# A transformer kernel's first layer: retention blocks moved between the k-tiles of the projections

## Chip, cores, metric

The kernel runs on one core of one Trainium2 chip. The metric is the device time in microseconds (us) of one execution; lower is better. It computes in f32, and all weights and activations come from HBM in one launch.

## What is computed

Four layers on 512 tokens of width 1024: two of a first block and two of a second. The change touches the first layer's mixer alone:

```
def _even_mixer(h, w_in, ret_norm_g, hg_norm_g, lb, w_out):
    rq, rk, rv, rg, gq, gf, gi, gg = _split_cols(h @ w_in, EV_SIZES)      # eight times 512 columns
    rq = _rotary(_split_heads(rq, RET_HEADS), pos)                        # 4 heads of 128
    rk = _rotary(_split_heads(rk, RET_HEADS), pos) * (RET_DK ** -0.5)
    ret = _retention_chunkwise(rq, rk, _split_heads(rv, RET_HEADS))
    ret = _merge_heads(_head_layer_norm(ret, ret_norm_g)) * jax.nn.silu(rg.astype(jnp.float32))
    hg = _hgrn2_chunkwise(_split_heads(gq, HG_HEADS), _split_heads(gf, HG_HEADS), _split_heads(gi, HG_HEADS), lb)
    hg = _merge_heads(_head_rms_norm(hg, hg_norm_g)) * jax.nn.silu(gg.astype(jnp.float32))
    y = jnp.concatenate([ret, hg], axis=-1).astype(h.dtype)
    return y @ w_out
```

The retention is `(q k^T * decay) v` over causal blocks of 128 tokens, then a layer norm per head (mean, centred value, mean square). The recurrence (hgrn2) uses forget gates `f = lb + (1 - lb) * sigmoid(gf)`, the running sum of their logarithm, and keys `1 - f`.

## The kernel before

**Units and jobs.** Weights come in units of 1024 x 256 (1 MB). SyncE loads a unit into one of two `raw` buffers; ScalarE (ACT) rounds it to `wH`; VectorE (DVE) subtracts (`wL = raw - wH`). TensorE (PE) then does three passes for each product, `hH wH`, `hL wH` and `hH wL` (`passes`): for a unit of 8 k-tiles and 2 output tiles that is 48 matmuls of 512 columns, called a job. In a token-major unit the operands are swapped: 96 matmuls of 256 columns. A job's result lies in one half of the PSUM tile `G` until DVE has read it (`job_free`). The `step` of ACT waits for the end of job n and rounds the unit of job n+2; the `step` of DVE reads the result of job n, then makes the `wL` of that unit. Every engine works strictly in the order in which its rows stand, and the semaphores that each row waits for are written by hand.

**The first layer's mixer.** Jobs 0 to 11 are twelve units of the projection: queries and keys (with rotary), values (token-major), retention gates RG, recurrent queries GQ, forget gates CUM. Then PE does the retention alone: 16 scores (`psS`, up to 512 columns, plain f32), each multiplied by the decay on DVE into `ws[SD]`, and 16 values blocks into `G`; per head the widths are 512, 384, 256 and 128. After that four means (a matmul with ones), four centred tiles on DVE, squares on ACT, and their sums per token (`stats`, 128x1 matmuls), DVE and GpSimd for the inverse root, four `spread`s (transposes that bring a column to all partitions), of which each needs its `columns` from DVE. Two token-major units of the recurrence's inputs GI stand before and behind the spreads. The level loop follows: 8 levels of recurrence blocks on `psS`, with two-matmul-tile pieces of the units GG between them.

**Bias rows.** After job 3, ACT issues a DMA that writes a table of 2560 KB to HBM for the second layer (`bias_out`).

Of the kernel before, what the change touches and what calls it, by code (L numbers as in the profile page):

```python
# [18 lines left out]
ALU = mybir.AluOpType  # L19
ACT = mybir.ActivationFunctionType  # L20
AX = mybir.AxisListType

P = 128
S = 512
# [165 lines left out]
def program(nc, a, out, scratch):  # L190
    ctx = contextlib.ExitStack()
    with ctx:
# [66 lines left out]
        MEMT, MH, ML = (0, 24), (4, 28), (8, 32)  # L259
        XOL, XOH = 0, 36  # L260
# [19 lines left out]
        for half in (8, 16, 32, 64, 128):  # L280
# [43 lines left out]
                                                     sem("rot_in"))  # L324
        b_done, b_read = sem("b_done"), sem("b_read")
        rs_done, rp_ready = sem("rs_done"), sem("rp_ready")
        mean_done, xc_ready = sem("mean_done"), sem("xc_ready")
# [38 lines left out]
        def _(sp):  # L366
# [16 lines left out]
            with sp.Fori(1, sum(UNITS_1) // 2) as i:  # L383
# [33 lines left out]
        def _(pe):  # L417
# [247 lines left out]
            for l in range(2):  # L665
                if l == 0:
                    for j in range(12):
                        if j == 0:
                            first_jobs(halves_in=True)
                        elif j in (4, 5):  # L670
                            token_major(h_op)
                        elif j > 1:
                            plain(h_op)
                        if j in (2, 3):
                            bias_rows(j - 2)

                    pe.wait_ge(b_read, 2)

                    pe.wait_ge(job_free, c.job.v + 2)
                    for s_ in range(18):  # L680
                        if s_ < 16:
                            h, jb = s_ // 4, s_ % 4

                            wait(pe, rp_ready, s_ - 1)
                            pe.matmul(psS[:, s_ % 2, 0:S - jb * P], ws[:, KR + h, jb * P:jb * P + P],
                                      ws[:, QR + h, jb * P:S], start=True, stop=True).then_inc(rs_done, 1)
                        r = s_ - 2
                        if r >= 0:
                            h, jb = r // 4, r % 4
                            pe.wait_ge(rp_ready, r + 1)  # L690
                            if r % 8 == 0:
                                take_job()
                            mm = pe.matmul(G[:, c.job.p * 2 + h % 2, jb * P:S], ws[:, V0 + jb, h * P:h * P + P],
                                           ws[:, SD + r % 3, 0:S - jb * P], start=(jb == 0), stop=(jb == 3))
                            if r % 8 == 7:
                                end_job(mm)


                    pe.wait_ge(job_free, c.job.v + 2)
                    for h in range(4):  # L700
                        wait(pe, xc_ready, h - 1)
                        pe.matmul(psS[:, h % 2, :], ones[:], ws[:, OS + h, :], start=True, stop=True)\
                            .then_inc(mean_done, 1)
                    pe.wait_ge(xc_ready, 4)
                    for m in range(2):
                        stats("tile", m, npairs=2)
                    token_major(h_op)
                    for h in range(4):
                        spread()
                    token_major(h_op)  # L710

# [425 lines left out]
        def _(act):  # L1137
# [187 lines left out]
            for l in range(2):  # L1325
                if l == 0:
                    for j in range(12):
                        step()
                        if j in (6, 7):
                            in_place(RG + 2 * (j - 6), ACT.Silu)  # L1330
                        elif j in (10, 11):
                            in_place(CUM + 2 * (j - 10), ACT.Sigmoid)
                        if j == 3:
                            bias_exps()
                    act.wait_ge(ln_in, 1)
                    activation(flat(CUM, 4), flat(CUM, 4), ACT.Ln).then_inc(ln_ready, 1)

                    c.job.off += 2
                    for m in range(2):
                        act.wait_ge(xc_ready, 2 * m + 2)  # L1340
                        square(ws[:, XC + 2 * m:XC + 2 * m + 2, :])
                    step()
# [3 lines left out]
                        .then_inc(t4_ready, 1)  # L1346
                    act.wait_ge(tn_ready, c.nrm.v + 4)
                    for h in range(4):
                        activation(ws[:, ZA + h, :], ws[:, CUM + h, :], ACT.Exp)
                        activation(ws[:, ZB + h, :], ws[:, CUM + h, :], ACT.Exp, scale=-1.0).then_inc(he_exp, 1)  # L1350
                    step()
                    step()
# [198 lines left out]
        def _(dve):  # L1551
# [348 lines left out]
            for l in range(2):  # L1900
                if l == 0:
# [31 lines left out]

                    for j in range(12):
                        if j < 4:
                            o = (QR, KR)[j // 2] + 2 * (j % 2)
                            step(rotary(ws[:, o:o + 2, :]))
                        elif j in (4, 5):
                            step(tokens(ws[:, V0:V0 + 4, (j % 2) * 256:(j % 2) * 256 + 256], 1))
                        elif j in (6, 7):  # L1940
                            step(by_rb(RG + 2 * (j - 6)))
                            c.ar.off += 1
                        elif j in (8, 9):
                            step(by_rb(GQ + 2 * (j - 8)))
                        else:
                            step(by_rb(CUM + 2 * (j - 10)))
                            forget(j - 10)
                        if j in (2, 3):
# [6 lines left out]
                    V.memset(tick[:], 0.0).then_inc(ln_in, 1)  # L1955
                    dve.wait_ge(table_in, 16)

                    n_out = 0
                    for s_ in range(17):
                        if s_ < 16:  # L1960
                            h, jb = s_ // 4, s_ % 4
                            w = S - jb * P
                            dve.wait_ge(rs_done, s_ + 1)
                            V.tensor_tensor(ws[:, SD + s_ % 3, 0:w], psS[:, s_ % 2, 0:w], ws[:, DEC + h, 0:w], ALU.mult)\
                                .then_inc(rp_ready, 1)
                        if s_ in (11, 16):
                            step(store(ws[:, OS + 2 * n_out:OS + 2 * n_out + 2, :]), unit=False)
                            n_out += 1
                    for h in range(4):
                        dve.wait_ge(mean_done, h + 1)  # L1970
                        V.scalar_tensor_tensor(ws[:, XC + h, :], psS[:, h % 2, :], -1.0 / P, ws[:, OS + h, :],
                                               ALU.mult, ALU.add).then_inc(xc_ready, 1)

                    def head_norm(src, gain, gate, to=None):
# [16 lines left out]

                    dve.wait_ge(ln_ready, 1)
                    for h in range(4):
                        ins = V.tensor_tensor_scan(ws[:, CUM + h, :], ws[:, RST, :], ws[:, CUM + h, :], 0.0,
                                                   ALU.mult, ALU.add)
                    ins.then_inc(scan_ready, 1)
                    head_norm(XC, lambda h: colx("ret", h), RG, RO)
                    inputs = lambda n: tokens(ws[:, GI:GI + 4, n * 256:n * 256 + 256], 1)
                    step(inputs(0))

                    for h in range(4):
                        dve.wait_ge(he_exp, h + 1)
                        V.tensor_tensor(ws[:, ZA + h, :], ws[:, ZA + h, :], ws[:, GQ + h, :], ALU.mult)
                        V.tensor_tensor(ws[:, ZB + h, :], ws[:, ZB + h, :], ws[:, KEY + h, :], ALU.mult)\
                            .then_inc(hz_ready, 1)
                    dve.wait_ge(t4_ready, 1)
                    for h in range(4):
# [597 lines left out]
```

## Time and profile before

| | |
|---|---|
| median of 3 runs | 3205.85 us (3205.09 to 3208.72) |
| profiled execution, its own time | 3207.22 us |
| its span in the profile | 3205.4 us |
| PE busy / weight loads | 3133.1 us (98%) / 2615.3 us (82%) |
| DVE / ACT / GpSimd busy | 1584.9 / 1075.8 / 290.4 us |
| granted clock of PE, mean | 0.987 |

The span is from the first to the last instruction. A matmul's row is as long as its way through the array, while matmuls come closer together than that; so the distance between starts counts, not the length. The clock is a share of 2.4 GHz.

### The profile page before, as it was taken

Reading aid. Unit: us, or ns where it says so; the run is one execution under the profiler, and the core shown is the slowest. Engines: PE = TensorE matmul, PEld = TensorE weight load, DVE = VectorE, ACT = ScalarE, POOL = GpSimd, SP = SyncE. Lnnn points to the kernel's source line nnn. Section 1 sums busy time; section 2 is a strip of 40 time slices with the busy share of each in tenths; the row PEclk is TensorE's granted clock in tenths of the full one; section 3 lists DMA queues with packets and bytes.
Section 4 is the critical chain, followed back from the end, with each engine's and each line's share of the span. In section 5 each row is a group of like instructions: output and inputs, shape, how many; then the busy total and the mean of one; then the engine's idle time right before and its main releaser. Section 6 shows DMA issues by size and latency. Waiting matters only on the chain.

```text
span 3205.4 us, 38813 instructions
## 1 busy us (share of the span) xinstructions
PE 3133.1 (98%) x15548; PEld 2615.3 (82%) x15548; DVE 1584.9 (49%) x1850; ACT 1075.8 (34%) x1166; POOL 290.4 (9%) x161
## 2 busy tenths in 40 slices
PE   9989999999999899999999999999999999999998
PEld 7778988888889798888888778888888777888887
DVE  7364644554334554455435755444433665444433
ACT  3212433443222443344323332333323342233322
POOL 0011200010000020011000300110100210101100
PEclk9999999999999999999999999999999999999999
DMA  4411411222232131122233122222222312222223
GB/s 167 123 40 48 140 63 66 105 92 105 105 107 92 35 136 67 66 93 104 94 113 104 66 71 100 92 96 101 92 107 97 93 66 101 97 92 92 95 105 115
DMA packets 47721, 299.92 MB, mean 94 GB/s; under 512 B 7091, under 2 KB 7347, under 8 KB 13284
## 3 DMA queue, kind: packets, MB, share of 16 engines
q1 hardware_dynamic: 42480, 288.01, 25.5%
q10 hardware_dynamic: 5108, 10.02, 1.3%
q8 instruction: 98, 1.61, 0.2%
q14 instruction: 35, 0.29, 0.0%
HBM read 293.26 MB, written 4.75 MB: 93 GB/s over the span
## 4 chain that ended last, share of the span: by engine, by line
PE 87%; DVE 6%; ACT 3%; issue 2%; DMA 2%; POOL 0%; ACTq 0%; DVEq 0%; SPq 0%
PE G L437 79%; DMA raw<-in_units 1%; DVE wL L1559 1%; ACT wH L1147 1%; PE psS L732 1%; PE psS L497 1%; DVE mxt L1766 1%; PE G L939 1%; DVE ws L2239 1%; PE psS L932 1%; PE psS L1030 1%; PE G L1039 1%; DVE ws L2236 0%; PE psT L529 0%; PE psS L488 0%
## 5 line engine op out<-in xcount | busy, mean ns | idle before, releaser
L437 PE MATMUL G<-hH,wH 128*128 128x512 f32 x2560 | 1016.3, 397 | 23.5 <-DVE wL L1559 7.9
L437 PE MATMUL G<-hL,wH 128*128 128x512 f32 x2560 | 1002.8, 392 | 0.0
L437 PE MATMUL G<-hH,wL 128*128 128x512 f32 x2560 | 1002.7, 392 | 0.0
L1559 DVE TENSOR_TENSOR wL<-raw,wH 128x2048 fp32r<-128x2048 f32 x265 | 637.7, 2406 | 663.7 <-ACT wH L1147 663.4
L437 PE MATMUL G<-wsr,wH 128*128 128x512 f32 (+1 forms) x2528 | 751.6, 381 | 2.0 <-DVE wsr L2105 0.9
L1147 ACT ACTIVATE wH<-raw 128x2048 fp32r<-128x2048 f32 x265 | 505.7, 1908 | 604.2 <-PE G L437 565.0
L437 PEld LDWEIGHTS G<-hH,wH 128*128 128x128 f32 x2560 | 484.6, 189 | 139.7 <-issue 16.3
L437 PEld LDWEIGHTS G<-hH,wL 128*128 128x128 f32 x2560 | 484.3, 189 | 102.8
L437 PEld LDWEIGHTS G<-hL,wH 128*128 128x128 f32 x2560 | 485.0, 189 | 98.0
L437 PEld LDWEIGHTS G<-wsr,wH 128*128 128x128 f32 x2528 | 466.8, 189 | 95.2 <-DVE wsr L2105 1.8
L437 PE MATMUL G<-wsr,wL 128*128 128x512 f32 (+1 forms) x1264 | 479.1, 379 | 0.0
L437 PEld LDWEIGHTS G<-wsr,wL 128*128 128x128 f32 x1264 | 238.4, 189 | 44.7
L2436 POOL TENSOR_TENSOR wsr<-sq,wsr 128x1024 f32 x44 | 105.8, 2405 | 841.3 <-ACT wsr L1264 841.3
L2414 POOL TENSOR_TENSOR rsb<-ms,neghalf 128x4 f32<-128x4 f32 (+4 forms) x21 | 37.6, 1790 | 1165.2 <-DVE ms L1602 1004.6
L1264 ACT ACTIVATE wsr<-sq 128x1024 f32 x44 | 46.7, 1062 | 231.4 <-DVE sq L1789 231.4
L1233 ACT ACTIVATE ws<-ws,mxt 128x128 f32<-128x128 f32 (+3 forms) x96 | 54.1, 564 | 207.3 <-DVE mxt L1766 206.8
L1713 DVE TENSOR_TENSOR x<-x,G 128x1024 f32<-128x1024 f32 x39 | 47.6, 1221 | 150.3 <-PE G L437 150.3
L437 PE MATMUL G<-wH,hH 128*128 128x256 f32 x384 | 113.5, 295 | 0.0
L437 PE MATMUL G<-wH,hL 128*128 128x256 f32 x384 | 109.8, 286 | 0.0
L437 PE MATMUL G<-wL,hH 128*128 128x256 f32 x384 | 109.7, 286 | 0.0
L1671 DVE TENSOR_TENSOR sq<-G,hmask 128x1024 f32<-128x1024 f32 x44 | 53.8, 1222 | 90.1 <-PE G L437 89.9
L1671 DVE TENSOR_TENSOR tn<-G,hmask 128x1024 f32<-128x1024 f32 x44 | 53.9, 1225 | 87.1 <-PE G L437 86.1
(272 smaller groups left out, 2591.2 us busy)
## 6 DMA issues: line engine op xcount, KB each, us to landing
raw<-in_units SPq DMA_DIRECT2D x265, 1024.0 KB, 4.8
ws<-bias_rows SPq DMA_DIRECT2D x2, 1536.0 KB, 14.7
bias_rows<-ws ACTq DMA_DIRECT2D x1, 2560.0 KB
x<-in_x SPq DMA_DIRECT2D x4, 512.0 KB, 7.9
ws<-in_mem ACTq DMA_DIRECT2D x2, 1024.0 KB, 4.8
ws<-bias_rows ACTq DMA_DIRECT2D x1, 2048.0 KB, 8.2
out_x<-x SPq DMA_DIRECT2D x4, 512.0 KB, 7.7
ws<-in_decay ACTq DMA_DIRECT2D x1, 1280.0 KB, 8.6
```

The source lines that it names most:

```text
L437: mm = pe.matmul(o, mv if swap else wt, wt if swap else mv, start=first and n == 0, stop=last and n == 2)
L497: mm = pe.matmul(st[:, col:col + 1], lhs, ones[:, 0:1], start=True, stop=True)
L732: mm = pe.matmul(psS[:, n % 2, o:o + w], k_[:, ks:ks + P], q_[:, qs:qs + w], start=True, stop=True)
L932: mm = pe.matmul(psS[:, r % 2, 0:M], ws[:, XQ + 2 * h + t, qt * P:qt * P + P], kx[:, 2 * h + t, :], start=(t == 0), stop=(t == 1))
L1147: activation(wH[:, g.p, :], raw[:, g.p, :], ACT.Copy).then_inc(wh_ready, 1)
L1233: return activation(p_, p_, ACT.Exp, bias=mxt[:, r % 4:r % 4 + 1], accum_out=den[:, r % 4:r % 4 + 1])
L1264: activation(aH[:, bass.ds(i * 2, 2), :], sq[:, 1], ACT.Copy).then_inc(ffn_h, 1)
L1559: V.tensor_tensor(wL[:, g.p, :], raw[:, g.p, :], wH[:, g.p, :].bitcast(F32), ALU.subtract)\
L1671: V.tensor_tensor(dst, g, rb_pair, ALU.mult).then_inc(job_free, 1)
L1713: V.tensor_tensor(x[:, 2 * jj:2 * jj + 2, :], x[:, 2 * jj:2 * jj + 2, :], g, ALU.add)\
L2414: W.tensor_tensor(dst[:, 0:cols], ms[:, 0:cols], neghalf[:].to_broadcast([P, cols]), ALU.pow)\
L2436: W.tensor_tensor(aL[:, bass.ds(i * 2, 2), :], sq[:, 1], aH[:, bass.ds(i * 2, 2), :].bitcast(F32), ALU.subtract).then_inc(ffn_ready, 1)
```

## The change

The order of the first layer's units becomes 0 to 5, 10, 11, 8, 9, 6, 7, 12 to 15: the forget gates are jobs 6 and 7, the recurrent queries 8 and 9, the retention gates 10 and 11. The retention no longer stands by itself. In jobs 6 to 9, after every second k-tile, there is a slot with one score and one value block; job 10's four slots hold the last two value blocks and the four means; job 11's second and third hold the sums of squares; the four spreads stand in the first of the two token-major units, after each token tile. The values go to `psT` instead of `G`, copied head by head, so there are two jobs fewer (68). Some temporary tiles are renumbered. On DVE and ACT the rows are put in the matching order.

```diff
-JOBS_1 = (70, 66)
+JOBS_1 = (68, 66)
+ORDER_1 = (0, 1, 2, 3, 4, 5, 10, 11, 8, 9, 6, 7, 12, 13, 14, 15)
-        ZA, ZB, DD, SX2, SX1, RO = 0, 4, 8, 12, 16, 39
+        ZA, ZB, DD, SX2, SX1, RO = 8, 35, 0, 12, 16, 39
@@ tensor
-                    for j in range(12):
+                    for j in range(6):
...
+                    def slotted(slot):
+                        take_unit()
+                        take_job()
+                        for k in range(KT):
+                            for t in range(2):
+                                w0 = k * 256 + t * P
+                                mm = passes(G[:, c.job.p * 2 + t, :], w0, w0 + P, h_op, k, slice(0, S),
+                                            k == 0, k == KT - 1)
+                            if k == KT - 1:
+                                end_job(mm)
+                            if k % 2 == 1:
+                                slot(k // 2)
+                        c.unit.off += 1
...
+                    def retained(s_):
+                        if s_ == 0:
+                            pe.wait_ge(b_read, 2)
+                            pe.wait_ge(job_free, c.job.v)
                         if s_ < 16:
                             h, jb = s_ // 4, s_ % 4
                             wait(pe, rp_ready, s_ - 1)
                             pe.matmul(psS[:, s_ % 2, 0:S - jb * P], ws[:, KR + h, jb * P:jb * P + P],
                                       ws[:, QR + h, jb * P:S], start=True, stop=True).then_inc(rs_done, 1)
                         r = s_ - 2
                         if r >= 0:
                             h, jb = r // 4, r % 4
                             pe.wait_ge(rp_ready, r + 1)
-                            if r % 8 == 0:
-                                take_job()
-                            mm = pe.matmul(G[:, c.job.p * 2 + h % 2, jb * P:S], ws[:, V0 + jb, h * P:h * P + P],
+                            if jb == 0 and h > 1:
+                                pe.wait_ge(os_ready, h - 1)
+                            mm = pe.matmul(psT[:, h % 2, jb * P:S], ws[:, V0 + jb, h * P:h * P + P],
...
+                    for j in range(4):
+                        slotted(lambda n: retained(4 * j + n))
+                    slotted(centred)
+                    slotted(squares)
@@ scalar
+                    for n in range(2):
+                        step()
+                        in_place(CUM + 2 * n, ACT.Sigmoid)
                     act.wait_ge(ln_in, 1)
                     activation(flat(CUM, 4), flat(CUM, 4), ACT.Ln).then_inc(ln_ready, 1)
-                    c.job.off += 2
+                    step()
+                    step()
+                    act.wait_ge(scan_ready, 1)
+                    activation(ws[:, RST, :], flat(CUM, 4).rearrange("p (n l) -> p n l", l=4)[:, :, 3], ACT.Exp)\
+                        .then_inc(t4_ready, 1)
                     for m in range(2):
                         act.wait_ge(xc_ready, 2 * m + 2)
                         square(ws[:, XC + 2 * m:XC + 2 * m + 2, :])
                     step()
+                    in_place(RG, ACT.Silu)
+                    act.wait_ge(os_ready, 4)
+                    act.wait_ge(bias_out, 16)
@@ vector
+                    for s_ in range(4):
+                        decayed(s_)
+                    step(by_rb(CUM))
+                    decayed(4)
+                    decayed(5)
+                    forget(0)
+                    decayed(6)
+                    retained(0)
+                    decayed(7)
+                    step(by_rb(CUM + 2))
...
+                    rstd(2, 16, P)
+                    first = c.bc.off
+                    columns(0)
+                    columns(4)
+                    step(by_rb(RG + 2))
```

How PE's rows stand shows it best. Before, where the retention begins: behind the last matmul of job 11 (line 437) come the scores (L685, from keys and queries in `ws` to `psS`) and the value blocks (L693, to `G`).

```order
L437 MATMUL G<-hH,wL 128x512
L685 MATMUL psS<-ws 128x512
L685 MATMUL psS<-ws 128x384
L685 MATMUL psS<-ws 128x256
L693 MATMUL G<-ws 128x512
L685 MATMUL psS<-ws 128x128
L693 MATMUL G<-ws 128x384
```

In the changed kernel the same place of the retention, score 2 and value block 0, stands in the third slot of job 6 (the unit's matmuls are line 443 there).

```order
L443 MATMUL G<-hH,wL 128x512
L707 MATMUL psS<-ws 128x256
L715 MATMUL psT<-ws 128x512
L443 MATMUL G<-hH,wH 128x512
L443 MATMUL G<-hL,wH 128x512
```

A pair of blocks that had only other blocks around it now has twelve matmuls of the unit before and after it.

DVE's rows in job 7 and its step. Before, the step (L1917 reads `G`, L1559 is the `wL` of the next unit but one) and the forget gates (L1928 to L1932) stand in one piece, ahead of all decay products (L1964).

```order
L1917 TENSOR_TENSOR ws<-G,tn 128x1024
L1559 TENSOR_TENSOR wL<-raw,wH 128x2048
L1928 TENSOR_SCALAR ws<-ws,lbt 128x512 x2
L1931 TENSOR_SCALAR ws<-ws 128x1024
L1932 TENSOR_SCALAR ws<-ws 128x1024
L1955 MEMSET tick 128x1
L1964 TENSOR_TENSOR ws<-psS,ws 128x512
L1964 TENSOR_TENSOR ws<-psS,ws 128x384
```

In the changed kernel, from the `wL` of unit 8 (L1614) to the `wL` of unit 9: decay products (L2008), forget gates (L1983 to L1987), a head's copy (L2014) and the step (L1972) alternate.

```order
L1614 TENSOR_TENSOR wL<-raw,wH 128x2048
L2008 TENSOR_TENSOR ws<-psS,ws 128x512
L2008 TENSOR_TENSOR ws<-psS,ws 128x384
L1983 TENSOR_SCALAR ws<-ws,lbt 128x512 x2
L1986 TENSOR_SCALAR ws<-ws 128x1024
L1987 TENSOR_SCALAR ws<-ws 128x1024
L2008 TENSOR_TENSOR ws<-psS,ws 128x256
L2014 COPY ws<-psT 128x512
L2008 TENSOR_TENSOR ws<-psS,ws 128x128
L1972 TENSOR_TENSOR ws<-G,tn 128x1024
L1614 TENSOR_TENSOR wL<-raw,wH 128x2048
```

The products of scores 4 and 5 stand behind the `wL` of unit 8, and those of 6 and 7 behind the forget gates.

## Rows read from the trace of the kernel before

**Rows 1.** The page: the chain that ended last, by engine.

```profile
PE 87%; DVE 6%; ACT 3%; issue 2%; DMA 2%; POOL 0%; ACTq 0%; DVEq 0%; SPq 0%
```

**Rows 2.** PE's waits, 60 to 345 us: total, times, longest.

```profile
PE psS L685 <- DVE ws L1964: 4.4, 1, 4.4
...
PE psT L529 <- DVE wide L1677: 2.0, 2, 1.2
```

**Rows 3.** PE in order of time, jobs 8 and 10: start, length, [idle before].

```profile
107.23 0.50 PE L437 MATMUL G<-hH,wH 128*128 128x512 f32 x1 [1.60 <-DVE wL L1559]
...
131.45 0.54 PE L437 MATMUL G<-hH,wH 128*128 128x512 f32 x1 [2.16 <-DVE wL L1559]
...
135.20 0.40 PE L437 MATMUL G<-hH,wH 128*128 128x512 f32 x1
```

**Rows 4.** PE in order of time, from job 11's end to the level loop.

```profile
154.72 0.39 PE L437 MATMUL G<-hH,wL 128*128 128x512 f32 x1
...
170.84 1.02 PE L685 MATMUL psS<-ws 128*128 128x512 f32 x2
...
175.16 1.02 PE L685 MATMUL psS<-ws 128*128 128x512 f32 x2
...
181.61 3.89 PE L702 MATMUL psS<-ws,ones 128*128 128x512 f32 x8 [1.32 <-DVE ws L1584]
186.28 3.81 PE L497 MATMUL psS<-ones,sq 128*128 128x1 f32 x32 [0.78 <-DVE ws L1971]
189.96 0.56 PE L437 MATMUL G<-wH,hH 128*128 128x256 f32 x1
...
202.75 0.28 PE L437 MATMUL G<-wH,hL 128*128 128x256 f32 x1
202.87 0.28 PE L437 MATMUL G<-wL,hH 128*128 128x256 f32 x1
...
207.31 0.56 PE L437 MATMUL G<-wH,hH 128*128 128x256 f32 x1
...
220.21 1.95 PE L732 MATMUL psS<-ws 128*128 128x128 f32 x16
```

**Rows 5.** Stretches: length, busy us (x) per engine, granted clock, DMA, GB/s.

```profile
83.69:94.57 10.88, 10.88 (x50) 9.01 (x49) 3.95 (x5) 1.92 (x1) 0.00 (x0) 1.00 0.71 143
...
131.00:144.00 13.00, 12.55 (x48) 10.26 (x49) 3.82 (x3) 1.91 (x1) 0.00 (x0) 0.87 0.45 163
190.00:222.00 32.00, 29.98 (x226) 29.50 (x226) 19.23 (x35) 10.11 (x12) 13.90 (x6) 0.90 0.10 34
```

**Rows 6.** PE in order of time, one cycle of the level loop.

```profile
228.72 1.95 PE L732 MATMUL psS<-ws 128*128 128x128 f32 x16
230.42 0.48 PE L437 MATMUL G<-hH,wH 128*128 128x512 f32 x1
...
231.88 1.95 PE L732 MATMUL psS<-ws 128*128 128x128 f32 x16
```

**Rows 7.** PE in order of time: sums and two spreads in the second layer.

```profile
961.43 1.84 PE L497 MATMUL psS<-ones,sq 128*128 128x1 f32 x16
963.13 1.07 PE L529 MATMUL psT<-ident,wide 128*128 128x128 f32 x8
963.95 0.47 PE L437 MATMUL G<-hH,wH 128*128 128x512 f32 x1
```

**Rows 8.** ACT and DVE in order of time, at the weights, a product, the columns.

```profile
102.93 1.92 ACT L1147 ACTIVATE wH<-raw 128x2048 fp32r<-128x2048 f32 x1 [17.05 <-DMA raw<-in_units]
127.15 1.92 ACT L1147 ACTIVATE wH<-raw 128x2048 fp32r<-128x2048 f32 x1 [17.18 <-DMA raw<-in_units]
...
104.88 2.29 DVE L1559 TENSOR_TENSOR wL<-raw,wH 128x2048 fp32r<-128x2048 f32 x1 [8.87 <-ACT wH L1147]
167.59 0.69 DVE L1964 TENSOR_TENSOR ws<-psS,ws 128x512 f32<-128x512 f32 x1 [1.21 <-PE psS L685]
193.79 0.24 DVE L1677 COPY wide<-rsb 128x4 f32<-128x4 f32 x2 [3.01 <-POOL rsb L2414]
```

More of the change, by code:

```diff
@@ L325, in program @@
         b_done, b_read = sem("b_done"), sem("b_read")
+        rv_done, os_ready = sem("rv_done"), sem("os_ready")
         rs_done, rp_ready = sem("rs_done"), sem("rp_ready")
@@ L382, in _ @@
                 sp.dma_start(dst, s_).then_inc(par_in, 16)
-            with sp.Fori(1, sum(UNITS_1) // 2) as i:
+            for n in range(2, len(ORDER_1)):
+                sp.wait_ge(wl_ready, n - 1)
+                sp.dma_start(raw[:, n % 2, :], a["units"][ORDER_1[n]]).then_inc(raw_in[n % 2], 16)
+            with sp.Fori(len(ORDER_1) // 2, sum(UNITS_1) // 2) as i:
                 for j in range(2):
@@ L699, in _, with mean @@
-                    pe.wait_ge(job_free, c.job.v + 2)
-                    for h in range(4):
-                        wait(pe, xc_ready, h - 1)
+                            if jb == 3:
+                                mm.then_inc(rv_done, 1)
+                    def mean(h):
+                        pe.wait_ge(os_ready, h + 1)
+                        if h < 2:
+                            pe.wait_ge(rp_ready, 16)
+                        else:
+                            pe.wait_ge(xc_ready, h - 1)
@@ L702, in _, with centred @@
                         pe.matmul(psS[:, h % 2, :], ones[:], ws[:, OS + h, :], start=True, stop=True)\
                             .then_inc(mean_done, 1)
[L704 to L710, printed above, removed]
+                    def centred(n):
+                        if n < 2:
+                            retained(16 + n)
+                        mean(n)
@@ new lines, in squares @@
+                    def squares(n):
+                        if n == 1:
+                            pe.wait_ge(xc_ready, 4)
+                        if 1 <= n <= 2:
+                            stats("tile", n - 1, npairs=2)
+                    for j in range(4):
[3 more added lines that the diff above has]
+                    for n in range(2):
+                        take_unit()
+                        take_job()
+                        for tt in range(ST):
+                            for k in range(KT):
+                                mm = passes(G[:, c.job.p * 2 + tt // 2, (tt % 2) * 256:(tt % 2) * 256 + 256],
+                                            k * 256, k * 256 + 256, h_op, k, slice(tt * P, tt * P + P),
+                                            k == 0, k == KT - 1, swap=True)
+                            if tt == ST - 1:
+                                end_job(mm)
+                            if n == 0:
+                                spread()
+                        c.unit.off += 1
@@ L1350, in _ @@
                         activation(ws[:, ZB + h, :], ws[:, CUM + h, :], ACT.Exp, scale=-1.0).then_inc(he_exp, 1)
+                    step()
+                    in_place(RG + 2, ACT.Silu)
+                    step()
                     step()
@@ L1932, in forget @@
                         c.link(V.tensor_scalar(f2, f2, F_FLOOR, None, ALU.max))
-                    for j in range(12):
+                    for j in range(6):
                         if j < 4:
@@ L1937, in _ @@
                             step(rotary(ws[:, o:o + 2, :]))
-                        elif j in (4, 5):
+                        else:
                             step(tokens(ws[:, V0:V0 + 4, (j % 2) * 256:(j % 2) * 256 + 256], 1))
[L1940 to L1947, printed above, removed]
                         if j in (2, 3):
@@ L1954, in _, with decayed, retained, scan @@
                             bias_sums()
[L1955 to L1969, printed above, removed]
+                    def decayed(s_):
+                        h, jb = s_ // 4, s_ % 4
+                        w = S - jb * P
+                        dve.wait_ge(rs_done, s_ + 1)
+                        V.tensor_tensor(ws[:, SD + s_ % 3, 0:w], psS[:, s_ % 2, 0:w], ws[:, DEC + h, 0:w], ALU.mult)\
+                            .then_inc(rp_ready, 1)
+                    def retained(h):
+                        dve.wait_ge(rv_done, h + 1)
+                        V.tensor_copy(ws[:, OS + h, :], psT[:, h % 2, :]).then_inc(os_ready, 1)
+                    def scan(h):
+                        return V.tensor_tensor_scan(ws[:, CUM + h, :], ws[:, RST, :], ws[:, CUM + h, :], 0.0,
+                                                    ALU.mult, ALU.add)
+                    def centred(h):
                         dve.wait_ge(mean_done, h + 1)
@@ L2005, in _ @@
                             .then_inc(hz_ready, 1)
+                    step(inputs(0))
                     dve.wait_ge(t4_ready, 1)
```

63 lines of the change are left out of this document (40 added, 23 removed).

## The prediction

> **What bounds the kernel now.** I read the chain of work that ended last first: 87% of it is TensorE (PE) [rows 1]. PE's busy share there is not news; what matters is what PE's time consists of where the change is made. So I next read who makes PE wait between 60 and 345 us, then PE's instructions in order of time, and at the end the other engines' rows at the places where PE waits.
>
> Two places lose time. The first is job 8 and job 10 of the first layer: PE waits 1.60 and 2.16 us for a low half of a weight unit (wL) [rows 3]. After the second wait the matmuls come slower: from 131.45 to 135.20 there are nine of them, 3.75 us, where a unit's 48 take 10.88 us, 0.227 each [rows 3, 5]. The granted clock of that stretch is 0.87, which is a mixture of the 1.2 and the 2.4 GHz level [rows 5]. Both waits are late weights: ScalarE (ACT) sat 17.05 and 17.18 us on the DMA of these raw units [rows 8], while the bias table was being written out.
>
> The second place is everything between job 11 and the level loop. Job 11's last matmul starts at 154.72, so the next could start at 154.95; the retention's scores and values, the means and the squares' sums run to 189.96; two token-major units with four spreads between them run to 220.21 [rows 4]. PE waits 4.4 us for the decay product of VectorE (DVE) [rows 2], 1.32 and 0.78 us at the start of the means and of the sums [rows 4], and 2.0 us for the columns of the spreads [rows 2]. The clock is 0.90 from 190 to 222 [rows 5]. All of it happens with no weight-unit work beside it: PE stands, or runs slowly, though six units of independent matmuls lie just before and two after.
>
> **The change, part by part.** The matmuls of the units, the scores, values, means, sums and spreads are all still there, of the same shapes. So I count what PE must do at full rate and what now lies around it.
>
> (a) Jobs 8 and 10. The unit loaded eighth still lands at about 102.9, since nothing on SyncE's queue changes before 88; its wL row starts 1.95 us after ACT's and lasts 2.29, so it is ready at 107.2 [rows 8]. Job 8 now starts later, because jobs 6 and 7 each carry four slots. A head's four scores and four values take 175.16 - 170.84 = 4.32 us [rows 4]. With four insertions at 0.10 (below) a slotted unit takes 10.88 + 4.32 + 0.4 = 15.6; job 6, which starts at 83.69 [rows 5], has no value block in its first two slots (384 columns, 0.65 us) and takes 14.9. So job 8 starts at about 83.7 + 14.9 + 15.6 = 114.2, 7 us after its weights. Unit 10's raw data landed at 127.15 [rows 8]; job 10 now starts near 146. Its cover is as deep. Removed: 1.60 + 2.16, and 3.75 - 9 x 0.227 = 1.71 of the slow stretch: **5.5 us**.
>
> (b) 154.95 to 189.96 is 35.01 us. What stays: four heads at 4.32 = 17.28; four means, each 512 columns like a score of jb 0, of which the 1.02 us row is the pipelined length; by the head's 2560 columns in 4.32 us, 512 columns are 0.86, together 3.45; two sets of sums at 963.13 - 961.43 = 1.70 each [rows 7], 3.40. Sum 24.1. Removed: **10.9 us**.
>
> (c) 189.96 to 220.21 is 30.25 us. What stays: 192 matmuls of 256 columns. At full rate they come every 0.12 us (two such rows stand in [rows 4], the last two of the first unit), 23.0; four spreads at (963.95 - 963.13) / 2 = 0.41 [rows 7], 1.6. Removed: 30.25 - 24.7 = **5.6 us**.
>
> (d) What it adds. PE now goes from a unit's matmuls to plain f32 ones and back 26 times: 16 slots with blocks, 4 with means (two with a block beside), 2 with sums, 4 spreads. The level loop already does this: block 1.70 us (230.42 - 228.72), then six unit matmuls, and a cycle of 3.16 (231.88 - 228.72) [rows 6]. 3.16 - 1.70 - 6 x 0.227 = 0.10 us for both turns. 26 x 0.10 = **2.6 us** to pay. Bounds: nothing (a turn hidden behind a 512-column stream), and a whole lost matmul place each, 0.227, or 5.9 us. I take the row, since it is the same pair of kinds.
>
> (e) The waits of the slots. On DVE the products (decayed), copies (retained) and the step of each job are now one line. The tightest wait is the third slot of job 7. Behind job 6's step stands the wL of unit 8, which waits for the late load; so from about 99.5 (job 6 ends at 97.6; one product and the step follow) DVE stands until 104.9, and the product of score 4 is queued behind it. It comes at 107.2 + 0.69 (a 512-column product [rows 8]) = 107.9. PE's score 6 and value 4, which need it, come at 83.7 + 14.9, three times two k-tiles of 2.72, and the two slots between at 1.4 and 0.9: 109.1. It fits by 1.2 us. In the later jobs the wL is done 4.3 us after the job's end and the product 5 us after it, and PE asks for it 11.5 us after: 6.5 us of slack. The spreads: today the first columns are ready 193.79 + 0.12 - 189.96 = 3.95 us after the sums end, most of it GpSimd's power (3.01) [rows 8]; now the sums end behind k-tile 5 of job 11, about 172, the columns are there at 176, and the first spread is asked for behind 24 matmuls of the next unit, at 178. Hidden, with 1.6 us left; the cover is two k-tiles and a token tile, and without it the 2 us of [rows 2] are back. ACT's exponentials, scans and table loads all move earlier and have the same units above them; the weights of job 12 wait behind the squares of the last means (about 161.3) and are ready at 166.6, needed at 175. I cost (e) at nothing. Two jobs fewer and the renumbered tiles move no work.
>
> **Sum.** 5.5 + 10.9 + 5.6 - 2.6 = 19.4 us less. The profiled execution took 3207.22 us with a span of 3205.4, which gives 3187.8 and a span of 3186.0; it lies 1.4 above the median of the runs, so against 3205.85 I predict **3186.5 us**. The level loop should start at about 201 in place of 220.2, and all after it is shifted unchanged.
>
> **Rivals.** *Slots that wait.* If the eighth load lands later than 102.9 by more than 1.2 us, DVE's product 4 is late and everything of PE is behind it. For it speaks that this load takes some 21 us today amid other traffic; against, that nothing before 88 is changed. Price: 2 to 3 us of waiting and one slow stretch of 1.7, and the like once more at the spreads: about 8 us, 3194.5.
>
> *The clock falls at sums or spreads.* Today the unit matmuls after the sums and after the spreads run at the low level [rows 4, 5]. Here it would be up to three stretches of 1.7: 5 us, 3191.5. Against it: in the second layer a set of sums and two spreads stand between unit matmuls for 2.52 us, and the next row is 0.47 long [rows 7], as after a block of the level loop (0.48) [rows 6]; after the wait at 131.45 it was 0.54 [rows 3].
>
> *Slower: the clock swings through the whole slotted stretch.* 26 times PE leaves the stream of unit matmuls. If more than 19.4 / 1.7 = 11 of these each left a slow stretch, the change would lose; with all 26 it is 44 - 19 = 25 us more, 3231. Against it speaks the level loop: whose turns leave the cycle at 3.16 us [rows 6]. For it, that those blocks are 1.70 us and of one kind, and that some slots wait on DVE. The Trainium skill has this as a rule (TensorE: Matmul & The Clock Gate, "A second HAM failure mode: psum-queue depth-cycling"): short idles between groups of matmuls can make the clock swing between its levels, and the throughput falls. By that rule the time would be this rival's; the level loop does not bear it out.
>
> *No change.* DVE becomes the bound: it would have to hold PE for 13 us in all, that is, the weights of two or three units would have to land later than the 6.5 us of slack. Then 3200 to 3206.
>
> **Chances.** The forecast, a gain of 17 to 22 us: 0.68. Late slots or slow stretches, 6.4 to 17 us: 0.23. No change: 0.05. Slower: 0.04. A change of 0.2% (6.4 us) is about what a measurement of this kernel can tell from none. Faster by that 0.91, within it 0.05, slower 0.04. The range: below, insertions that cost nothing (2.6) and 1.5 us for what the median may be off: 3182.5; above, both middle rivals' lesser forms, and turns at 0.227 (3.3 more) with one wait: 3194.
>
> **What would show it.** Right: no PE wait on wL at jobs 8 and 10; score and value blocks every 2.72 us plus their own length; level loop from about 201; 0.10 at each turn. The forecast is wrong if the slots' rows carry waits on the decay products (e), if unit matmuls after sums or spreads are longer than 0.40 us, if the turns cost more (d), or if the stretch behind the level loop changes its length.

## The result, and the profile after

The changed kernel takes 3180.89 us (3179.68 to 3183.21, 4 runs), the kernel before 3206.17 us (3205.09 to 3208.72, 4 runs): a ratio of 0.9924, with an interval of 0.9908 to 0.9940. That is 25.3 us faster, where 19.4 were forecast, and 1.6 us below the lower end of the range. The direction and the place were right; the forecast gain was too small.

The granted clock and the waits are where the difference shows first. In the profile after, PE's three largest waits from 60 to 345 us are these (total, times, longest):

```profile
PE psS L782 <- DVE ws L2137: 1.9, 1, 1.9
PE psS L494 <- ACT sq L1213: 1.4, 1, 1.4
PE G L443 <- POOL hL L2519: 0.9, 1, 0.9
```

These three were there before too; the 1.9 us stands behind the start of the level loop. Nothing is left of [rows 2] or of the two waits of [rows 3]. Stretches of the same profile: length, busy time (instructions) of PE, weight loads, DVE, ACT and GpSimd, granted clock, DMA share, GB/s.

```profile
83.69:199.28 115.59, 115.59 (x605) 95.11 (x604) 64.03 (x84) 36.51 (x30) 5.39 (x6) 1.00 0.38 102
199.28:330.00 130.72, 125.11 (x731) 109.75 (x730) 73.61 (x121) 37.76 (x45) 21.52 (x19) 0.96 0.16 58
1736.00:1873.00 137.00, 129.14 (x764) 100.85 (x764) 93.72 (x171) 50.15 (x99) 29.00 (x16) 0.99 0.20 70
```

From job 6 to the level loop PE is busy for all of the 115.59 us, and its clock is 1.00, where [rows 5] had 0.87 and 0.90. The loop starts at 199.28 and not at 220.21 [rows 4]: 20.9 us. The spans of the two profiles differ by 27.4 us (3205.4 and 3178.0). So 6.5 us of this pair arose behind the loop's start, where no row was changed. That is the question for the experiments.

Job 6, with which the changed part begins, does not start at the same time in every execution. In the profile before it starts at 83.69 [rows 5], in this one at 84.08:

```profile
84.08 0.40 PE L443 MATMUL G<-hH,wH 128*128 128x512 f32 x1
```

So the sharper measure of the change is the distance from job 6's first row to the loop's first row: 136.52 us before, 115.20 after, 21.3 us less.

PE's rows in order of time show the slots, two of them one job apart:

```profile
93.86 0.59 PE L707 MATMUL psS<-ws 128*128 128x256 f32 x2
94.29 1.02 PE L715 MATMUL psT<-ws 128*128 128x512 f32 x2
...
109.21 0.59 PE L707 MATMUL psS<-ws 128*128 128x256 f32 x2
109.64 1.02 PE L715 MATMUL psT<-ws 128*128 128x512 f32 x2
...
124.99 1.02 PE L715 MATMUL psT<-ws 128*128 128x512 f32 x2
```

A job with its four slots takes 109.64 - 94.29 = 15.35 us and the next one 15.35 again; its matmuls alone are 10.88 + 4.32 = 15.20. The tight place was job 7's third slot. ACT and DVE have it so:

```profile
103.34 1.92 ACT L1197 ACTIVATE wH<-raw 128x2048 fp32r<-128x2048 f32 x1 [17.07 <-DMA raw<-in_units]
...
105.29 2.29 DVE L1614 TENSOR_TENSOR wL<-raw,wH 128x2048 fp32r<-128x2048 f32 x1 [5.52 <-ACT wH L1197]
107.50 1.15 DVE L2008 TENSOR_TENSOR ws<-psS,ws 128x512 f32<-128x512 f32 x2
```

ACT still idles 17.07 us for the late load, as in [rows 8], but its unit is not asked for until 114. The first of the two products is done at about 108.2 (107.50 and 0.69), and PE asks for it at 109.21: 1.0 us of slack, where 1.2 were worked out.

### The profile page after: what moved, and what is told of

It reads as the page before. It is cut to its first block, busy times and chain, and to the rows that moved or that the text cites. A ratio compares the mean times of both kernels' runs of the same rounds, so it can differ in the third digit from the quotient of the medians.

```text
span 3178.0 us, 38774 instructions
## 1 busy us (share of the span) xinstructions
PE 3118.1 (98%) x15548; PEld 2603.7 (82%) x15548; DVE 1584.6 (50%) x1852; ACT 1076.7 (34%) x1167; POOL 281.8 (9%) x161
## 4 chain that ended last, share of the span: by engine, by line
PE 90%; DVE 5%; ACT 2%; issue 2%; DMA 0%; POOL 0%; DVEq 0%; ACTq 0%; SPq 0%
PE G L443 82%; ACT wH L1197 1%; DVE wL L1614 1%; PE psS L782 1%; DVE mxt L1821 1%; PE psS L503 1%; PE psS L982 1%; PE G L989 1%; DVE ws L2336 1%; PE psS L1080 1%; PE G L1089 1%; DVE ws L2333 0%; PE psT L535 0%; PE psT L1116 0%; PE G L1007 0%
## 5 line engine op out<-in xcount | busy, mean ns | idle before, releaser
L1614 DVE TENSOR_TENSOR wL<-raw,wH 128x2048 fp32r<-128x2048 f32 x265 | 637.5, 2406 | 647.3 <-ACT wH L1197 646.9
```

Source lines behind the costliest of these rows:

```text
L1614: V.tensor_tensor(wL[:, g.p, :], raw[:, g.p, :], wH[:, g.p, :].bitcast(F32), ALU.subtract)\
```

## The experiments

Each series gives the kernel's own median beside runs of the kernel before on the same chip. One execution of either kernel scatters by about 2.4 us (standard deviation), so a series of five is good to some 2 us. The rows of the profiles are much sharper, and most verdicts rest on them: the time from job 6's first row to the level loop's first row, and what lies behind the latter (the span less its start). All in us:

| profile | job 6 | loop | between | behind |
|---|---|---|---|---|
| before | 83.69 | 220.21 | 136.52 | 2985.2 |
| before_again | 83.71 | 220.02 | 136.31 | 2985.1 |
| before_bias_late | 84.37 | 213.51 | 129.14 | 2987.5 |
| after | 84.08 | 199.28 | 115.20 | 2978.7 |
| after_again | 83.75 | 198.95 | 115.20 | 2984.9 |
| after_third | 83.79 | 199.00 | 115.21 | 2978.3 |
| pad12 | 84.25 | 202.14 | 117.89 | 2981.4 |
| pad24 | 83.85 | 204.42 | 120.57 | 2980.1 |
| unit_ends | 83.91 | 201.93 | 118.02 | 2986.5 |
| sums_apart | 83.68 | 207.03 | 123.35 | 2980.5 |
| every_k | 84.65 | 200.36 | 115.71 | 2978.5 |
| split_later | 83.92 | 199.13 | 115.21 | 2983.0 |
| split_later_again | 83.81 | 199.02 | 115.21 | 2977.0 |

Up to the loop each kernel repeats itself, within 0.01 us for the changed one and 0.2 for the one before. Behind it the same program varies by 6.6 us.

**The changed kernel again (after_again).** No edit.

> The changed kernel once more, for a tight ratio and a second profile. The first two profiles put the level loop at 199.28 instead of 220.21, 20.9 us earlier, and the end 27.4 us earlier; 6.4 us of it arose behind the level loop, where nothing was changed: at the memory's sums in layers 1 and 2 (a set of 32 rows took 6.96 us before and 4.92 after) and at the start of the third layer's attention (granted clock 0.95 before, 0.99 after). Theory A (where the low clock falls is chance): the level loop starts at 199.3 again, the low stretches behind it lie elsewhere in this profile, and the difference of the medians comes down towards 21, say 21 to 25 us. Theory B (the shift by 21 us itself sets where they fall, the same way in each run): 25 us again, with the low stretches at the same rows.

3182.83 us (3178.92 to 3185.83), ratio 0.9927 (0.9914 to 0.9941). The loop starts at 198.95, and the span is 3183.8. What lies behind the start took 2984.9 us here, 2978.7 in the first profile, and 2985.2 in the kernel before. The memory's sums (start, length, idle before) in the first profile and in this one:

```profile
1085.86 4.92 PE L494 MATMUL psS<-ones,sq 128*128 128x1 f32 x32 [2.90 <-ACT sq L1213]
```

```profile
1086.61 6.95 PE L494 MATMUL psS<-ones,sq 128*128 128x1 f32 x32 [2.51 <-ACT sq L1213]
```

They are the same 32 rows, 2.03 us longer: the granted clock over them is 0.73 in the first profile and 0.50 in this one, so the low clock covers about half of them in one execution of the program and all of them in the other. The third layer's attention, in this second profile:

```profile
1736.00:1873.00 137.00, 130.75 (x754) 101.93 (x754) 93.67 (x171) 52.28 (x101) 28.99 (x16) 0.95 0.17 62
```

0.95 here and 0.99 above. Behind the loop Theory A holds for the low stretches: they are not at the same rows each time. The difference of the medians in this series is 22.7 us, inside Theory A's 21 to 25.

**The kernel before again (before_again).** No edit.

> The kernel before, unchanged, for a second profile. The write of the bias table done late moved the level loop from 220.21 to 213.51 us in its profile, but the medians by 3.4 us alone. Theory A (the low stretches of the clock fall by chance, in the changed part too): the level loop of this second profile starts somewhere from 217 to 221, the waits are the same, and the end minus the loop's start is 2985 within 4 us. Theory B: 220.2 again within 0.3 us, and the low stretches stand at the same rows.

3204.96 us (3202.68 to 3209.68), ratio 1.0001 (0.9991 to 1.0011). The loop starts at 220.02, the rest takes 2985.1 us. In the changed part the kernel before repeats itself within 0.2 us, the low stretches included: Theory B for this part. Behind the loop the sum is the same by chance, since its parts are not: between the same two wL rows of the first layer it took 156.5 in one profile and 155.0 in the other, in the second layer's attention 185.1 and 182.8, in the fourth layer's 58.4 and 61.6.

**Known work added (pad12, pad24).**

```diff
                         if n == 1:
                             pe.wait_ge(xc_ready, 4)
+                            for _ in range(12):          # 24 in pad24
+                                pe.matmul(psS[:, 1, 0:P], ident[:], ones[:], start=True, stop=True)
```

> The changed kernel with 12 extra plain f32 matmuls of 128 columns on PE in job 11's second slot, that is 12 x 0.213 = 2.6 us of known work that nothing hides, and all behind it shifted by that. It adds work and changes no output. Theory A: 2.6 us slower than the changed kernel, within the scatter of 1.5 us. Theory B (position sets the low stretches): the low stretches behind the level loop move to other rows, and the time is off from +2.6 by 1 to 5 us. Rival C (slack hides it: something behind the level loop waits for other things than PE): less than 1 us slower.

> The same with 24 extra matmuls, 5.1 us. Theory A: 5.1 us slower than the changed kernel within 1.5 us. Theory B: off from that by 1 to 5 us, and by another amount than with 12. Rival C: well below 5 us.

3185.33 us (3184.08 to 3190.58) and 3189.36 us (3186.26 to 3194.66). From job 6 to the loop it is 2.7 and 5.4 us more than in the changed kernel, as 2.6 and 5.1 were expected. Over its 14 runs of all series the changed kernel has a mean of 3181.6; the pads have 3186.6 and 3190.2, so 5.0 and 8.6 more. Rival C is out: no slack behind the loop hides PE's work there. The 2.3 and 3.2 us beyond the shift have standard errors of 1.4 and 1.7, so they are not established by the times. A low stretch that the changed kernel does not have stands in pad24's profile, at the second pair of blocks of the level loop. These 16 rows take 2.94 us there and 2.02 in all three profiles of the changed kernel, and the next pair follows 1.6 us later than there:

```profile
209.69 2.94 PE L784 MATMUL psS<-ws 128*128 128x128 f32 x16 [1.93 <-DVE ws L2139]
```

At this place the profile speaks for Theory B, that the position sets the low stretch. It is one profile, but the changed kernel's three repeat these rows within 0.02 us.

**The bias table late, in the kernel before (before_bias_late).** The DMA is issued behind the logarithm of job 11.

```diff
+            def bias_write():
                 act.wait_ge(bias_row, 1)
                 act.dma_start(scratch.rearrange("h (p w) -> h p w", w=E_W + 1)[:, :, 0:E_W], ...)
...
                     activation(flat(CUM, 4), flat(CUM, 4), ACT.Ln).then_inc(ln_ready, 1)
+                    bias_write()
```

> The kernel before, with the write of the bias table issued behind the logarithm at job 11 and not behind job 3; all else as it was. It does term (a) alone, by another way. Theory: the raw units of jobs 8 and 10 land in time, the waits of 1.60 and 2.16 us and the slow stretch of 1.71 us behind the second go away: 5.5 us faster than before, about 3200.5. Rival: the waits come from something else than this DMA (the two weight buffers' turn), and the time stays; or the late table makes the weights of jobs 14 and 15 late, and the gain is given back at the level loop.

3202.07 us (3198.43 to 3204.62, 11 runs), ratio 0.9990 (0.9981 to 0.9999). ACT in order of time now takes the units without a wait for a DMA:

```profile
95.56 1.92 ACT L1147 ACTIVATE wH<-raw 128x2048 fp32r<-128x2048 f32 x1 [8.99 <-PE G L437]
...
106.44 1.92 ACT L1147 ACTIVATE wH<-raw 128x2048 fp32r<-128x2048 f32 x1 [6.59 <-PE G L437]
...
117.32 1.92 ACT L1147 ACTIVATE wH<-raw 128x2048 fp32r<-128x2048 f32 x1 [8.02 <-PE G L437]
```

Both waits of [rows 3] are gone, and from job 6 to the loop it is 7.4 us less than in the kernel before. Six units take 65.3 us here and took 71.3, which is (a): 6.0. Nearly all of the rest, 1.3, is the low stretch behind the spreads, which did not occur in this profile. So the write did make these loads late. The time fell by 3.2 us only (means 3202.1 and 3205.4). Part of the gain is given back at the second pair of blocks of the level loop:

```profile
219.78 3.58 PE L732 MATMUL psS<-ws 128*128 128x128 f32 x16 [2.93 <-DVE ws L2043]
```

PE waits 2.93 us for the masks where it waited 1.93, and the rows, 3.58 us long in place of 2.02, run at a granted clock of 0.54. That is 2.6 of the missing 4.2 us. No weights are late there, so the rival's cause is not what is seen.

**Slots at the unit's end (unit_ends).**

```diff
-                            if k % 2 == 1:
-                                slot(k // 2)
+                        for n in range(4):
+                            slot(n)
                         c.unit.off += 1
```

> The changed kernel with its four slots of a unit moved behind the unit's last k-tile: the same blocks, means and sums, in the same jobs, but in one piece at each unit's end. Theory 1 (what counts is that late weights and DVE's steps have a unit of other work above them; the fineness counts nothing): the number of turns falls by some 18, which at 0.04 each is 0.7 us, against small waits between neighbouring blocks for the decay product; the time stays within 2 us of the changed kernel. Theory 2 (the fine interleaving is what hides the round trip PE to DVE and back): a product takes 0.69 us and the blocks follow each other by 0.85 us or less, so each unit's end loses 2 to 4 us, and the whole is 8 to 16 us slower than the changed kernel.

3186.13 us (3182.22 to 3190.23), ratio 0.9938 (0.9924 to 0.9951); the loop starts 2.8 us later behind job 6 than in the changed kernel, and the mean is 3186.5, 4.9 us above its 3181.6. Neither number was met: it is more than Theory 1's 2 us and less than Theory 2's 8. PE's rows in order of time name the losses:

```profile
144.87 0.49 PE L707 MATMUL psS<-ws 128*128 128x128 f32 x2 [0.89 <-DVE ws L2008]
...
172.13 3.63 PE L503 MATMUL psS<-ones,sq 128*128 128x1 f32 x32
...
176.69 0.42 PE L443 MATMUL G<-wL,hH 128*128 128x256 f32 x1
```

Two waits for a product make 1.1 us. The sums stand together for 3.6 us, and 15 matmuls behind them come every 0.21 us and not every 0.12 (0.42 long and not 0.28): 1.4 us. Behind the loop's start the low clock falls on the second pair of blocks too (3.6 us long for 2.0), as in pad24. Most of the change's gain needs only that each job carries a share of the retention: 18.4 of the 21.2 us. Spreading the share over the job's k-tiles adds the last 2.8 us.

**Sums and spreads together again (sums_apart).** Job 11 has no slots, its sums and all four spreads stand behind their units.

```diff
-                    slotted(squares)
+                    plain(h_op)
+                    pe.wait_ge(xc_ready, 4)
+                    for m in range(2):
+                        stats("tile", m, npairs=2)
...
-                            if n == 0:
-                                spread()
+                        if n == 0:
+                            for h in range(4):
+                                spread()
```

> The changed kernel with term (c) undone: the sums of squares stand behind job 11 in one piece and the four spreads behind the first token-major unit in one piece, as before; the retention keeps its slots. Forecast by (c): up to 5.6 us slower than the changed kernel: 2.0 us of waits for the columns come back, the rest is the low clock behind the sums and behind the spreads. Rival (c is the clock alone, and the clock stays high here since the sums have unit work before them and no idle): 2 to 3 us slower, from the waits of the spreads alone.

3189.38 us (3185.18 to 3196.87), ratio 0.9955 (0.9942 to 0.9969). The loop starts 8.1 us later behind job 6. PE in order of time, and the stretch from 165 to 207:

```profile
170.48 4.63 PE L503 MATMUL psS<-ones,sq 128*128 128x1 f32 x32
174.98 0.56 PE L443 MATMUL G<-wH,hH 128*128 128x256 f32 x1
...
190.98 0.65 PE L535 MATMUL psT<-ident,wide 128*128 128x128 f32 x4 [1.29 <-DVE wide L1736]
...
193.63 1.12 PE L535 MATMUL psT<-ident,wide 128*128 128x128 f32 x4 [2.01 <-DVE wide L1736]
```

```profile
165.00:207.00 42.00, 38.70 (x265) 37.25 (x265) 21.44 (x33) 12.33 (x14) 5.38 (x6) 0.88 0.18 62
```

3.3 us are waits for columns, about 1 the sums (4.5 us for 3.4 at full rate), and 31 slow matmuls behind sums and spreads at 0.093 each make 2.9. The rival, that the clock would stay high behind a full unit, fell: it is 0.88, though no idle stood before the sums. In this trace, as in that of unit_ends, the low clock comes with the 32 sums in one piece or behind them, without a wait of PE ahead.

**A slot behind each k-tile (every_k).** The score goes behind the even k-tile, the value block or the mean behind the odd one.

```diff
-                            if k % 2 == 1:
-                                slot(k // 2)
+                            slot(k // 2, k % 2)
...
-                        if s_ < 16:
+                        if s_ < 16 and part == 0:
...
-                        if r >= 0:
+                        if r >= 0 and part == 1:
```

> The changed kernel with the score of a slot behind its first k-tile and the value block (or the mean) behind its second: 18 turns more between unit matmuls and plain f32 ones, the same work. It measures the price of a turn. By the changed kernel's own profile a head of four slots takes 15.34 us where its matmuls alone take 10.88 + 4.32 = 15.20, so a turn costs 0.035 us: the level loop 0.6 us later, the time the same within 1.5 us. By the 0.10 of the prediction it would be 1.8 us later. Rival (many turns make the clock fall): low stretches between jobs 6 and 11, and 5 us or more slower.

3180.89 us (3180.28 to 3183.41), ratio 0.9928 (0.9914 to 0.9941). The loop starts at 200.36, but job 6 had started late already, at 84.65, before any of the edit. Between the two are 115.71 us, 0.5 more than in the changed kernel: the 0.6 that its own profile gave, and not the 1.8 of the prediction. The edit adds 16 turns and not 18 (42 in the trace, where the changed kernel has 26), so 0.03 each at most. Of the 0.5, 0.4 arose in job 7, where score 6 is now asked for one k-tile earlier and has to wait for the product of score 4 (done at 107.96 + 0.69):

```profile
107.96 1.15 DVE L2008 TENSOR_TENSOR ws<-psS,ws 128x512 f32<-128x512 f32 x2
```

```profile
108.70 0.70 PE L706 MATMUL psS<-ws 128*128 128x256 f32 x2
```

The matmul before it starts at 108.24, so it could have started at 108.47. Job 7's third slot is the one that the prediction called the tightest; here its 1.0 us of slack is used up. The clock did not fall:

```profile
83.69:200.36 116.67, 116.61 (x610) 95.61 (x609) 64.10 (x84) 36.52 (x30) 5.39 (x6) 1.00 0.38 102
```

42 turns leave it at 1.00.

**The changed kernel a third time (after_third).** No edit.

> The changed kernel a third time. In its two profiles the stretch behind the level loop's start took 2978.7 and 2984.9 us, in the kernel before 2985.2 and 2985.1. If these are chance, the loop starts at 199.1 within 0.3 us, the stretch lies anywhere from 2978 to 2988, and the median is 3182 within 1.5 us, so that the gain is 21 to 25 us. If the changed kernel were faster there by itself, it would be 2979 again.

3179.64 us (3179.13 to 3184.71), ratio 0.9927 (0.9914 to 0.9941). The loop starts at 199.00, as expected; behind it are 2978.3 us, the short value again. The median is 2.4 us below the expected 3182, the gain in this series 24.8 us. Neither branch fits alone: the value was 2979 again, and yet one of the changed kernel's three profiles has 2985.

**The last low half later (split_later, split_later_again).** DVE makes the wL behind the second token-major unit after level 0's masks.

```diff
-                    step(inputs(1))
+                    step(inputs(1), unit=False)
...
+                        if lev == 0:
+                            split()
                         if lev == 5:
                             dve.wait_ge(bias_out, 16)
```

> The changed kernel, in which DVE makes the low half of the last unit's weights (the 2.29 us row behind the second token-major unit) after the four masks of level 0 and not before them. The one wait of PE left from job 6 to the loop's second block is 1.93 us for these masks. Theory: that wait goes, PE starts the third block 1.9 us earlier, and the time is 1.9 us lower, within what can be measured of 1.5. Rival: the half is then late for its own unit, or DVE is late in level 1 by the same 2.3 us, and nothing is gained.

> The version with the last low half behind the masks once more, beside the changed kernel on the same chip. It was 3179.59 us, the changed kernel 3182.83 in an earlier series. If the 1.93 us wait is the whole of it, it is 1.9 us below after_third, within 1.5; if it is nothing, both are alike.

3179.59 us (3178.17 to 3183.89) and 3180.12 us (3177.83 to 3186.60), ratios 0.9919 (0.9905 to 0.9932) and 0.9930 (0.9916 to 0.9943). In PE's rows the second pair of blocks now follows without a wait:

```profile
199.13 1.95 PE L782 MATMUL psS<-ws 128*128 128x128 f32 x16
200.83 0.47 PE L443 MATMUL G<-hH,wH 128*128 128x512 f32 x1
...
202.30 1.95 PE L782 MATMUL psS<-ws 128*128 128x128 f32 x16
```

The wait is gone in the trace, and with it 2.1 us. The fifth pair of blocks gives back 0.45; the last pair of the level loop starts 1.7 us earlier behind job 6 (162.3 and 162.4 us, for 164.0) in both profiles. In the time it is not established: the ten runs have a mean of 3180.8 against 3181.6 of the changed kernel, 0.8 with an error of about 1.1, and beside after_third the version was not faster.

## Why the prediction was right, and where it failed

**The waits and low stretches from job 6 to the loop** were the gain, as forecast. Between these two rows lie 136.52 and 136.31 us in the profiles of the kernel before, and 115.20, 115.20 and 115.21 in those of the changed one: 21.2 us, shown, against 19.4. The 1.8 us more are in (d) and (a).

**(a)** was 5.5 us and is 6.0: six units took 71.3 us (83.69 to 154.95) and take 65.3 at full rate, as before_bias_late shows with its 65.3. The prediction counted the two waits and one slow stretch; the rest is some 0.15 us before or behind each of the waits.

**(b)** 10.9 us was not tried by itself. It is what remains of the 21.2, and the trace before has most of it in rows: the waits of 4.4, 1.5, 1.3 and 0.8 us, of which the prediction does not name the 1.5, and a low stretch right behind the longest of them, which it does not name either. The granted clock there (the third number from the end) is 0.51:

```profile
162.60:166.00 3.40, 3.31 (x7) 2.10 (x8) 0.93 (x3) 1.30 (x1) 0.00 (x0) 0.51 0.37 154
```

**(c)** 5.6 us: undone alone it costs 8.1. The mechanism was right (columns and low clock); in the experiment both the columns' wait (3.3, not 2.0) and the sums themselves are longer than before. From the first token-major unit to the loop the changed kernel takes 24.7 us, as counted.

**(d)** is the term that was mis-sized. Six units, the four heads, means, sums, two token-major units and spreads make 65.3 + 17.3 + 3.45 + 3.4 + 23.0 + 1.6 = 114.1 us, and the changed kernel takes 115.2. So 26 turns cost 1.1 us, 0.04 each, and every_k has at most 0.03; the prediction took 0.10 from the level loop, 2.6 in all. 1.5 of the 1.8 us missing up to the loop are here.

**(e)** nothing: shown. No slot waits, with 1.0 us of slack at the tightest one, and every_k shows what happens without it; the spreads' columns are hidden.

**"All after it is shifted unchanged"** is the step that failed. Over all series the kernels have means of 3205.4 (51 runs) and 3181.6 us (14 runs): 23.7 us apart, with a 95% interval of about 1.5. 21.2 of them are up to the loop, 2.5 behind it, where the prediction had nothing. In the recorded profile pair it was 6.5, and the 25.3 us of the recorded medians are 1.6 above the 23.7: that part is luck of the runs. Even the mean of 3181.6 lies below the range's 3182.5.

What differs behind the loop is the granted clock. Each run has its mean on record. Seven of the changed kernel's 14 runs have 0.992, and they took 3178.92 to 3179.92 us; the other seven have 0.989 to 0.991 and took 3181.94 to 3185.83. The kernel before took 3201.36 to 3202.39 in the five runs with 0.990 and 3209.68 to 3210.08 in the four with 0.986, of 47. The low stretches that the change removed are worth 0.002 of the mean (an estimate: 0.05 of 136.52 us, over 3205), so its 0.990 compares with 0.992: five of 47 against seven of 14. With the interval of 1.5, the 2.5 us are not chance alone. The changed kernel meets the shorter pattern of low stretches more often, and pad24's one profile says that a shift can bring such a stretch. Why this position is the better one stays open. The range allowed 1.5 us for all of this, too little for a kernel whose single executions differ by up to 8.7.

**The rivals.** Slots that wait and a DVE bound did not occur. The slower one (a swinging clock) fell: the granted clock is 1.00 with 26 turns and with 42. The Trainium skill's passage on it (TensorE: Matmul & The Clock Gate, "A second HAM failure mode: psum-queue depth-cycling") speaks of short idles between the groups of matmuls; here PE had none, so its case did not arise. "The clock falls at sums" did not occur at two sets of 1.8 us with two k-tiles between them; unit_ends and sums_apart show that it does occur with the 32 rows together. It is real, and in these traces it is absent where the change spaces them out.

## What to carry to other kernels

A stage that one engine runs alone loses more than its waits: count the low-clock rows behind them too. Put its blocks between pieces of independent matmuls; one share per job gave 18.4 of the 21.2 us here, four shares per job the rest. Longer jobs also hide late loads. Measure from the first row of the changed part and not from zero: job 6's start varies by 1.0 us over these profiles, and in every_k that would have made a turn more than twice as dear. When a profile pair shows more than the changed rows explain, profile the unchanged kernel twice before explaining it.

## What the runs showed of the hardware

The stretch behind the change comes in steps. Between two wL rows in the third layer's attention, the changed kernel took 22.13 us in one execution and 23.74 in another:

```profile
1752.48 2.29 DVE L1614 TENSOR_TENSOR wL<-raw,wH 128x2048 fp32r<-128x2048 f32 x1 [0.96 <-ACT wH L1197]
1774.61 2.28 DVE L1614 TENSOR_TENSOR wL<-raw,wH 128x2048 fp32r<-128x2048 f32 x1
```

```profile
1754.89 2.29 DVE L1614 TENSOR_TENSOR wL<-raw,wH 128x2048 fp32r<-128x2048 f32 x1 [0.96 <-ACT wH L1197]
1778.63 2.28 DVE L1614 TENSOR_TENSOR wL<-raw,wH 128x2048 fp32r<-128x2048 f32 x1
```

From some 240 us on, 233 of the 249 distances from one wL row to the next repeat within 0.25 us over all 13 profiles. Some eight take one of two or three values that lie 1 to 3 us apart. The one shown here is 23.7 to 24.0 us in all three profiles of the kernel before or its variant, and in three of the ten of the changed kernel and its variants; in the other seven it is 22.1. That is where most of the scatter of this kernel comes from.

A row's low clock is not always behind an idle engine. In unit_ends and sums_apart PE had no wait ahead of the 32 sums, and the granted clock fell during or behind them (0.88 from 165 to 207 us in sums_apart).
